# Cached keys through a bfloat16 copy and transposing DMAs, an earlier K^T for the first head, and eight PSUM banks for the first gate

## The chip, the cores and the metric

The program runs on the 8 cores of one Trainium2 chip, each core by itself: there is no traffic between them. The time is the device time of the slowest core, in microseconds. Each of the four prompt streams is shared by a pair of cores. The even core of a pair (role 0) owns the first 19 blocks of 128 frames and the two sample streams of the pair. The odd core (role 1) owns the last 13 blocks and recomputes the keys and values of the 19 before. Only the even cores hold cached keys.

## The reference, cut to what matters

```python
h = rmsnorm(x);  z = h @ w_in                 # columns: q | k | v | f | g_A | u | v_B | g_B
# A) forgetting attention, 8 heads x 128
logf = log_sigmoid(z_f + b_f);  cum = cumsum(logf)
s = (q @ k.T) * 128**-0.5 + cum[t] - cum[s];  p = softmax(causal(s));  att = p @ v
#    sample rows (16 per stream): k, v and logf are the 2048 cached rows, then the new ones
# B) gMLP: gelu(u) * (tril(W_s) @ LN(gelu(v_B)) + b), per 128-chunk and channel group
y = x + concat(att * silu(g_a), B * silu(g_B)) @ w_out;  y = rmsnorm(y)
```

The outputs are y, k, v, logf of prompt and sample rows and the sample's normalised v_B. Inputs are float32; matmul operands are bfloat16.

## The kernel before, in words

`emit` writes the instructions of one role by hand, engine by engine. Each engine executes its own list in order, and semaphores tie the lists. A DMA issued by SP or by POOL waits, in that queue, for its semaphores; what is listed behind it waits too. Only POOL's DMAs cast; the transposing DMAs (`tload`, line 131 of the helper) are all on SP. PSUM has 8 banks; `next_bank` hands them out in turn from the range in `banks`.

The stages of an even core, with `no` = 19 blocks and `ns` = 2 sample streams:

1. **K and V** (up to about 350 us): norm, transposes, K and V of each block. K goes to a bfloat16 scratch `K_s` in DRAM, row by row, V to `V_s`.
2. **v_B** (`b_front`, `b_back`, to about 510 us): v_B of each block, kept in SBUF as `vn`.
3. **The chunks** (`for ci in range(1, 17)`): 16 column chunks of w_in, alternately u and g_B of a channel group, each 80 matmuls (L581). The weights come by POOL's casting DMAs into a ring of 4 slots, so that a load is issued four chunks ahead. After each u chunk `mixing(gi - 1)` does a channel group's 128-chunk mixing: 19 matmuls (L860) and one for the sample rows (L868), in 6 calls of `next_bank` (banks 0 to 5), and on DVE three operations for each of them (L876, L877, L879); SP stores the result (`oT_s`).
4. **Crossing to attention**: `mixing(7)`; the attention's buffers are placed (`take_kv`, a write to a place waits for the earlier users of it); `e_loads(0)` on SP fetches the first head's K^T (transposing DMAs from `K_s`, 2432 and 32 rows) and V; POOL fetches the cached rows of both streams, `kc_load` and `vc_load`, 2048 rows of 128 float32 each, cast on the way; then the first head's gate, `ga_groups`: 20 blocks in 5 groups of 64 matmuls (L945), each group in one bank, evicted by ACT (tanh, L957) and DVE (L959). Here `banks` is set to 6 and 7. SP then fetches the query-side sums of the first two tiles (`cq_load`, from `CQ_s`), which DVE's diagonal step (L1156) reads.
5. **Attention**: per head a list of units, `hu`: 50 off-diagonal and 19 diagonal ones in six query tiles (4, 3, 3, 3, 3, 3 blocks), and 8 for the samples: `ktc0`, `ktc1` (8 PE transposes each of the cached K, L1118, and a DVE copy, L1164, to `KTc`), `smpS` (16 score matmuls, L1124) and `smpO` (16 matmuls, L1133, and a short DVE chain). Scores rotate through banks 0 to 2; the products with V (L1213) follow 5 units later (`LPV`) into bank 3 for off-diagonal and bank 4 for diagonal units; 7 units later (`LACC`) `fin_acc` reads them (L1081, L1084, L1086). Among the units of head h, `fill_upto` spreads 402 pieces of filler: the q projection (80 matmuls, L581) and the gate (320, L945) of head h + 1, with two ring loads. The last head has no filler. Loads for head h + 1 are issued at fixed unit positions: K^T and V at 9, the cached rows at 4, 18, 40 and 54.
6. **Output**: at the first unit of head 7 POOL issues the 16 loads of w_out (`wo_loads`), into the place of the dead H; near the head's end SP fetches the mixed rows (`g_load`, `oT_s` as it is and `o_s` by a transposing DMA). Then 1280 matmuls (L1336) and the final norm.

The lines that fix what the change touches:

```python
banks.update(lo=6, hi=8)                                   # before the first gate
for pos, kd, i in ((0, "ktc0", 0), (1, "ktc1", 0), (8, "smpS", 0), (14, "smpO", 0),
                   (36, "ktc0", 1), (37, "ktc1", 1), (44, "smpS", 1), (50, "smpO", 1)):
    hu.insert(pos, dict(kind=kd, h=h, st=i))
if u["pos"] == 9 and h + 1 < 8: e_loads(h + 1)
for pos, ld, st_ in ((4, kc_load, 0), (18, vc_load, 0), (40, kc_load, 1), (54, vc_load, 1)): ...
```

Of the kernel before, what the change touches and what calls it, by code (L numbers as in the profile page):

```python
# [137 lines left out]
class Chip:  # L138


    def __init__(self):
# [65 lines left out]
def emit(C, role):  # L207
# [674 lines left out]

    EB = W0 + 2 * QS + 2 * QS + 4096 + 512
# [219 lines left out]
    def e_S(i):  # L1103
# [5 lines left out]
        if k in ("off", "diag"):  # L1109
# [4 lines left out]
                  reads=[R_KTh[p], R_Qh[p]], writes=[PSR[bk]])  # L1114
        elif k in ("ktc0", "ktc1"):
            half = int(k[3])
            for j in range(8):
                PE.op(lambda j=j: nc.tensor.transpose(PSB[bk][:, :].bitcast(BF16)[:, j * 128:(j + 1) * 128], kc[u["st"]][:, half * 8 + j, :], S["ident_b"][:, :]),  # L1118
                      reads=[R_kc[u["st"]], R["ident_b"]], writes=[PSR[bk]] if j == 0 else [], pwrites=[] if j == 0 else [PSR[bk]], sig=(j == 7))
        elif k == "smpS":  # L1120
            c0 = no * 128 + u["st"] * NS
# [17 lines left out]
    def e_soft(i):  # L1139
# [5 lines left out]
        if k in ("off", "diag"):  # L1145
# [324 lines left out]
```

How the kernel before makes its waits and increments, by code:

```python
    def _wait(self, ev):  # L68
        sem, val = ev
        if sem is self.sem and self.is_pe:
            return
        if self.seen.get(id(sem), 0) >= val:
            return
        self.eng.wait_ge(sem, val)
        self.seen[id(sem)] = val
# [32 lines left out]
    def op(self, fn, reads=(), writes=(), pwrites=(), sig=True):  # L108
        self._deps(reads, writes, pwrites)
        ins = fn()
        if sig:
            ins.then_inc(self.sem, 1)
            self.cnt += 1
            ev = (self.sem, self.cnt)
        else:
            ev = (self.sem, self.cnt + 1)
        self._update(ev, reads, writes, pwrites)
        return ev
# [1 line left out]
    def dma(self, out, in_, dsem, reads=(), writes=(), pwrites=()):  # L120
        self._deps(reads, writes, pwrites)
        self.eng.dma_start(out=out, in_=in_).then_inc(dsem.sem, 16)
        dsem.cnt += 16
        ev = (dsem.sem, dsem.cnt)
        self._update(ev, reads, writes, pwrites)
        return ev
# [1 line left out]
    def dmat(self, out, in_, dsem, reads=(), writes=(), pwrites=()):  # L128
        self._deps(reads, writes, pwrites)
        self.eng.dma_start_transpose(out=out, in_=in_).then_inc(dsem.sem, 16)
        dsem.cnt += 16
        ev = (dsem.sem, dsem.cnt)
        self._update(ev, reads, writes, pwrites)
        return ev
```

## Time and profile before

| | |
|---|---|
| median of 3 runs | 1607.96 us (1606.09 to 1791.97) |
| the profiled execution | 1603.71 us, span 1600.1 us (core 2) |
| even cores | 1596.8, 1600.1, 1599.0, 1598.4 us |
| odd cores | 1564.7, 1561.2, 1562.9, 1561.4 us |
| busy on core 2 | PE 95 %, ACT 40 %, DVE 38 %, POOL 15 % |
| costliest lines | L581 419.1 us, L1336 278.7, L945 216.7, L1151 (ACT) 210.1, L1213 176.8, L1113 173.7 |

The profile is of core 2, the slowest. A busy time counts a matmul from its start to its modelled end, and matmuls overlap, so the time from one start to the next is what PE pays. In a timeline, "x128" merges 128 like instructions and the bracket gives the idle time before the first of them and what ended it. Line numbers are those of the kernel before.

### The profile page before, as it was taken

How to read it: one execution, taken by the hardware profiler on the slowest of the kernel's cores; microseconds unless marked ns; L12 is line 12 of the kernel's file. 1: busy time of each engine (PE TensorE's matmuls, PEld its weight loads, DVE VectorE, ACT ScalarE, POOL GpSimd, SP SyncE). 2: the span in 40 equal slices, each digit the busy share in tenths (PEclk: the TensorE clock that was granted, in tenths of full speed). 3: DMA queues.
4: the chain of work that ended last, by engine and by line, in shares of the span. 5: the costliest groups of instructions: out<-in, count | busy, mean ns of one | idle time of the engine just before them, and what ended most of it. 6: DMA issues, size and time to landing. Idle time of an engine off the chain costs nothing.

```text
span 1600.1 us, 31906 instructions; the slowest of 8 cores (1561.2 to 1600.1 us)
## 1 busy us (share of the span) xinstructions
PE 1515.2 (95%) x11367; PEld 887.4 (55%) x11367; DVE 600.4 (38%) x1276; ACT 642.5 (40%) x1331; POOL 247.1 (15%) x361
## 2 busy tenths in 40 slices
PE   3899999999999999999989999999999879999998
PEld 1455556554444444444568678677687644444443
DVE  1323222104444023322434445444444534544444
ACT  1222322214565222222227566566565652333332
POOL 5111111140333100000021212221111300000000
PEclk9999999999999999999999999999999899999999
DMA  9965445296000334333398877958846798756752
GB/s 188 232 196 179 178 168 181 109 191 80 1 1 1 40 43 56 44 58 49 50 161 109 117 90 111 116 68 122 102 68 97 122 225 210 226 151 207 188 160 90
DMA packets 266853, 191.38 MB, mean 120 GB/s; under 512 B 224762, under 2 KB 236194, under 8 KB 261634
## 3 DMA queue, kind: packets, MB, share of 16 engines
q1 hardware_dynamic: 125378, 134.69, 30.1%
q0 software_dynamic: 141312, 54.57, 29.7%
q8 instruction: 96, 1.57, 0.4%
q14 instruction: 67, 0.55, 0.1%
HBM read 172.85 MB, written 60.84 MB: 146 GB/s over the span
## 4 chain that ended last, share of the span: by engine, by line
PE 88%; DMA 6%; DVE 1%; ACT 1%; issue 1%; POOL 1%; another core or an unknown queue 0%; SPq 0%; POOLq 0%; DVEq 0%; ACTq 0%
PE psb L581 25%; PE psb L1336 17%; PE psb L785 9%; PE psb L440 8%; PE psb L430 8%; PE psb L945 7%; PE psb L1213 5%; PE psb L1113 5%; DMA arena<-w_in 2%; DMA o_s<-arena 1%; POOL arena L122 1%; PE psb L1133 1%; PE psb L415 1%; DMA arena<-oT_s 1%; DMA arena<-x_own 1%
## 5 line engine op out<-in xcount | busy, mean ns | idle before, releaser
L581 PE MATMUL psb<-arena 128*128 128x496 bf16 (+1 forms) x1920 | 419.1, 372 | 3.2 <-ACT psb L795 2.8
L581 PEld LDWEIGHTS psb<-arena 128*128 128x128 bf16 x1920 | 183.7, 98 | 194.8 <-issue 6.4
L1336 PE MATMUL psb<-arena 128*128 128x512 bf16 (+1 forms) x1280 | 278.7, 381 | 3.7 <-DMA arena<-oT_s 3.7
L1151 ACT ACTIVATE arena<-psb,offb 128x384 bf16<-128x384 f32 x400 | 210.1, 582 | 51.6 <-PE psb L1113 41.2
L945 PE MATMUL psb<-arena 128*128 128x128 bf16 (+1 forms) x2560 | 216.7, 220 | 4.3 <-DVE arena L959 4.3
L1336 PEld LDWEIGHTS psb<-arena 128*128 128x128 bf16 (+1 forms) x1280 | 125.6, 98 | 156.4 <-issue 7.1
L1213 PE MATMUL psb<-arena 128*128 128x129 bf16 x1520 | 176.8, 221 | 14.2 <-DVE arena L1081 7.9
L1113 PE MATMUL psb<-arena 128*128 128x384 bf16 (+3 forms) x552 | 173.7, 315 | 8.1 <-ACT arena L1151 3.7
L945 PEld LDWEIGHTS psb<-arena 128*128 128x128 bf16 (+1 forms) x2560 | 164.0, 98 | 11.9 <-issue 4.4
L430 PE MATMUL psb<-arena 128*128 128x512 bf16 (+1 forms) x640 | 147.4, 389 | 21.8 <-DMA arena<-w_in 15.4
L440 PE MATMUL psb<-arena 128*128 128x344 bf16 (+1 forms) x960 | 146.1, 311 | 7.0 <-DMA arena<-w_in 3.0
L1213 PEld LDWEIGHTS psb<-arena 128*128 128x128 bf16 x1520 | 124.1, 98 | 49.1 <-issue 17.0
L785 PE MATMUL psb<-arena 128*128 128x512 bf16 (+1 forms) x640 | 138.6, 379 | 0.0
L598 ACT ACTIVATE arena<-psb 128x496 bf16<-128x496 f32 (+1 forms) x120 | 69.3, 577 | 167.4 <-PE psb L581 166.4
L440 PEld LDWEIGHTS psb<-arena 128*128 128x128 bf16 (+1 forms) x960 | 93.4, 98 | 54.9 <-issue 10.0
L1361 ACT ACTIVATE arena<-arena 128x512 bf16<-128x512 f32 (+1 forms) x80 | 50.3, 629 | 175.2 <-DVE arena L1359 175.2
L430 PEld LDWEIGHTS psb<-arena 128*128 128x128 bf16 (+1 forms) x640 | 63.3, 99 | 99.7 <-issue 30.6
L1156 DVE SCALAR_TENSOR_TENSOR arena<-psb,cumn,arena 128x128 f32<-128x128 f32 (+3 forms) x152 | 74.2, 496 | 100.9 <-PE psb L1213 79.9
L122 POOL DMA_DIRECT2D arena<-w_in x80 | 64.4, 850 | 274.6 <-PE psb L860 124.6
L785 PEld LDWEIGHTS psb<-arena 128*128 128x128 bf16 (+1 forms) x640 | 62.4, 98 | 76.1 <-issue 1.2
L1159 ACT ACTIVATE arena<-arena 128x128 bf16<-128x128 f32 (+3 forms) x152 | 63.6, 426 | 95.8 <-DVE arena L1156 90.2
L876 DVE TENSOR_TENSOR arena<-psb,arena 128x512 f32<-128x512 f32 (+2 forms) x48 | 27.8, 579 | 185.3 <-PE psb L860 185.3
(151 smaller groups left out, 1202.7 us busy)
## 6 DMA issues: line engine op xcount, KB each, us to landing
arena<-x_own SPq DMA_DIRECT2D x38, 1024.0 KB, 6.9
y_own<-arena SPq DMA_DIRECT2D x38, 512.0 KB, 4.7
arena<-w_in POOLq DMA_DIRECT2D x32, 512.0 KB, 6.5
k_own<-arena SPq DMA_DIRECT2D x19, 512.0 KB, 3.7
v_own<-arena SPq DMA_DIRECT2D x19, 512.0 KB, 2.8
arena<-w_in POOLq DMA_DIRECT2D x32, 256.0 KB, 15.7
arena<-ck POOLq DMA_DIRECT2D x16, 512.0 KB, 8.0
arena<-cv POOLq DMA_DIRECT2D x16, 512.0 KB, 8.8
```

The lines of the kernel that those rows point to most:

```text
L122: self.eng.dma_start(out=out, in_=in_).then_inc(dsem.sem, 16)
L430: PE.op(lambda k=k, c=c: mm(PSB[2 + c][0:rows, :], hT[:, k, :], WK[:, k, c * 512:(c + 1) * 512], start=(k == 0), stop=(k == KC - 1)), read ...
L440: PE.op(lambda k=k, c=c: mm(PSB[4 + c][0:rows, 0:VC], hT[:, k, :], WV[:, k, c * VC:(c + 1) * VC], start=(k == 0), stop=(k == KC - 1)), rea ...
L581: PE.op(lambda: mm(PSB[bk][:, 0:n], wt[:, k, :], H[:, k, c0:c0 + n], start=(k == 0), stop=(k == KC - 1)), reads=rh + [r_wt], writes=[PSR[b ...
L598: ACT.op(lambda: act(out=dst[:, c0:c0 + n], in_=PSB[bk][:, 0:n], func=func), reads=[PSR[bk]], writes=[r_dst] if ti == 0 else [], pwrites=[ ...
L785: PE.op(lambda k=k, c=c: mm(PSB[pb + c][0:rows, :], H[:, k, c0:c0 + rows], WVB[k][:, c * 512:(c + 1) * 512], start=(k == 0), stop=(k == KC ...
L945: PE.op(lambda: mm(PSB[bk][0:rows, jj * 128:(jj + 1) * 128], H[:, k, j * 128:j * 128 + rows], wt[:, k, :], start=(k == 0), stop=(k == KC - ...
L1113: PE.op(lambda: mm(PSB[bk][:, o:o + n], KTh[p][:, gk * 128:(gk + 1) * 128], Qh[p][:, q0 + o:q0 + o + n], start=True, stop=True), reads=[R_ ...
L1151: ACT.op(lambda: act(out=Pb[pi][:, 0:n], in_=PSB[bk][:, 0:n], func=AF.Exp, scale=SCALE, bias=S["offb"][:, t["oo"] + u["g"], h:h + 1]), rea ...
L1156: DVE.op(lambda: v.scalar_tensor_tensor(out=dt[di][:, 0:n], in0=PSB[bk][:, o:o + n], scalar=S["cumn"][:, t["b0"] + u["i"], h:h + 1], in1=c ...
L1213: PE.op(lambda: mm(PSB[bk][:, c0:c0 + 129], Pb[pi][:, a * 128:(a + 1) * 128], Vh[p][:, u["g"], 0:129], start=first, stop=True, skip_group_ ...
L1336: PE.op(lambda: mm(PSB[bk][0:rows, :], oT[op_][:, k, j * 128:j * 128 + rows], wo[k][:, cg * 512:(cg + 1) * 512], start=(ki == 0), stop=(ki ...
```

## The change

- In the chunks 1 to 8, POOL copies a quarter of one stream's cached K (512 rows of 1024, float32) to a new scratch `kc_s` in DRAM, cast to bfloat16: eight copies, on even cores alone.
- `kc_load` becomes a transposing DMA on SP from `kc_s` straight to `KTc`, which now has one buffer for each stream; the units `ktc0` and `ktc1` go (four units in each of the 8 heads), with their buffers `kc`. The `smpS` units move to the head's start (0 and 1; in the first head 12 and 13), the `smpO` units to 20 and 26; the loads move to 15, 16 (K) and 28, 40 (V).
- `e_loads` is split. The first head's K^T, `KTh0`, has a place of its own and is fetched after chunk 12.
- The first gate takes all eight banks, from bank 6 on (6, 7, 0, 1, 2); the narrowing to banks 6 and 7 follows it.
- The attention's buffers are placed in another order, and on odd cores the last w_out rows and the output buffers move.

```diff
+        self.kc_s = dscr("kc_s", [NSMAX * PAST, 1024], BF16)
...
-    bsb, R_bsb = b.take("bsb", [128], F32)
-    assert b.off <= W0 + 32768
+    EA = b.off
+    KTh0, R_KTh0 = b.take("KTh0", [nk * 128 + NR], BF16)
+    EK = b.off
+    assert EK <= W0 + 32768
...
+    def e_kloads(h):
+        p = h % 2
+        tload(KTh[p][:, 0:nk * 128].unsqueeze(1), C.K_s[0:nk * 128, h * 128:(h + 1) * 128], R_KTh[p], extra=[R_Ks])
+        if ns:
+            tload(KTh[p][:, nk * 128:nk * 128 + NR].unsqueeze(1), C.K_s[NKEY:NKEY + NR, h * 128:(h + 1) * 128], R_KTh[p], extra=[R_Ks], part=True)
...
         ring_load()
+        if ci == 12:
+            e_kloads(0)
+        if ns and ci <= ns * 4:
+            r0 = (ci - 1) * (PAST // 4)
+            POOL.dma(C.kc_s[r0:r0 + PAST // 4, :], C.ck[r0:r0 + PAST // 4, :], dsem_of(R_kcs), pwrites=[R_kcs])
...
     mixing(7)
-    banks.update(lo=6, hi=8)
-    take_kv(0)
+    banks.update(lo=0, hi=8, n=6)
...
+    assert b.off <= EA
+    b.off = EK
+    take_v(0)
...
+        KTc, R_KTc = b.many("KTc", ns, [PAST], BF16)
...
-    e_loads(0)
+    e_vloads(0)
 
     def kc_load(h, i):
-        load(POOL, kc[i][:, :, :], C.ck[i * PAST:(i + 1) * PAST, h * 128:(h + 1) * 128].rearrange("(b t) c -> t b c", t=128), R_kc[i])
+        tload(KTc[i][:, :].unsqueeze(1), C.kc_s[i * PAST:(i + 1) * PAST, h * 128:(h + 1) * 128], R_KTc[i], extra=[R_kcs])
...
     for f in ga_groups(ring[17 % NSLOT], R_ring[17 % NSLOT], GAh[0], R_GAh[0]):
         f()
+    banks.update(lo=6, hi=8)
     ring_load()
...
-            for pos, kd, i in ((0, "ktc0", 0), (1, "ktc1", 0), (8, "smpS", 0), (14, "smpO", 0),
-                               (36, "ktc0", 1), (37, "ktc1", 1), (44, "smpS", 1), (50, "smpO", 1)):
+            for pos, kd, i in ((12 if h == 0 else 0, "smpS", 0), (13 if h == 0 else 1, "smpS", 1), (20, "smpO", 0), (26, "smpO", 1)):
...
-        elif k in ("ktc0", "ktc1"):
-            half = int(k[3])
-            DVE.op(lambda: v.tensor_copy(out=KTc[:, half * 1024:(half + 1) * 1024], in_=PSB[bk][:, :].bitcast(BF16)),
-                   reads=[PSR[bk]], writes=[R_KTc] if half == 0 else [], pwrites=[] if half == 0 else [R_KTc])
...
             if u["pos"] == 9 and h + 1 < 8:
-                e_loads(h + 1)
+                e_kloads(h + 1)
+                e_vloads(h + 1)
             if ns and h + 1 < 8:
-                for pos, ld, st_ in ((4, kc_load, 0), (18, vc_load, 0), (40, kc_load, 1), (54, vc_load, 1)):
+                for pos, ld, st_ in ((15, kc_load, 0), (16, kc_load, 1), (28, vc_load, 0), (40, vc_load, 1)):
```

## Rows read from the trace of the kernel before

**Rows 1.** Spans and granted clock of the cores, one odd and the slowest even.

```profile
core 1: 1564.7 us, clock 0.991
...
core 2: 1600.1 us, clock 0.988
```

**Rows 2.** Chain of waits, core 2, 817 to 1260: shares by line, two head starts.

```profile
by line: PE psb L581 26.3%; PE psb L945 26.2%; PE psb L1213 17.1%; PE psb L1113 16.0%; PE psb L1133 3.3%; PE psb L1118 3.0%; issue 1.9%; ACT arena L957 1.3%; PE psb L1124 1.2%; ACT arena L1151 0.9%; DVE arena L1081 0.9%; DVE arena L1156 0.4
...
1133.63 1.26 PE psb L581 x6
...
1197.07 1.26 PE psb L581 x6
```

**Rows 3.** Timeline, core 2, the last head and the first output matmuls.

```profile
1260.77 8.51 POOL L122 DMA_DIRECT2D arena<-w_out  x16 [0.24 <-issue]
...
1270.01 0.59 PE L1213 MATMUL psb<-arena 128*128 128x129 bf16 x4 [4.18 <-POOL arena L1160]
...
1314.27 2.29 PE L1336 MATMUL psb<-arena 128*128 128x512 bf16 x5 [3.66 <-DMA arena<-oT_s]
```

**Rows 4.** DMA queues, core 2, 1260 to 1316 (queue: packets, MB, share).

```profile
DMA packets 9203, 11.64 MB, mean 208 GB/s; under 512 B 5611, under 2 KB 7147, under 8 KB 9195
...
q0 software_dynamic: 2304, 8.39, 76.5%
```

**Rows 5.** Timeline, core 2, last mixing and first gate (start us, us, engine line op).

```profile
791.40 7.32 PE L945 MATMUL psb<-arena 128*128 128x128 bf16 x128
...
801.39 0.18 DVE L876 TENSOR_TENSOR arena<-psb,arena 128x32 f32<-128x32 f32 x1
...
802.15 1.28 DVE L959 SCALAR_TENSOR_TENSOR arena<-arena,psb 128x512 bf16<-128x512 f32 x2
...
802.98 12.61 PE L945 MATMUL psb<-arena 128*128 128x128 bf16 x192 [4.26 <-DVE arena L959]
...
816.95 0.61 PE L1118 MATMUL psb<-ident_b,arena 128*128 128x128 bf16 x8 [1.36 <-DMA arena<-ck]
```

**Rows 6.** Windows, core 2 (stretch, length, busy by engine, PEclk, DMA share, GB/s).

```profile
668.00:703.00 35.00, 35.00 (x183) 17.01 (x182) 10.09 (x18) 8.37 (x12) 2.28 (x2) 1.00 0.37 49
...
802.00:817.00 15.00, 12.66 (x193) 12.44 (x194) 3.36 (x6) 1.68 (x3) 6.71 (x11) 0.89 1.11 161
```

**Rows 7.** Chain of waits, core 2, 1197 to 1320: one transpose unit.

```profile
1198.33 0.45 PE psb L1118 x8
```

**Rows 8.** Line 131, core 2: issue time on SP of each transposing load.

```profile
L131 SPq DMA_TRANSPOSE arena<-K_s x16: 1205/1824/8440, 803.1 to 1212.7; - x16
```

**Rows 9.** DMA issues, core 2 (count, KB each, median us to landing).

```profile
arena<-ck POOLq DMA_DIRECT2D x16, 512.0 KB, 8.0
...
arena<-K_s SPq DMA_TRANSPOSE x16, 4.7
```

**Rows 10.** Timeline of SP's DMA queue, core 2: issues at 803 to 814 and 893.

```profile
803.06 5.66 SPq L131 DMA_TRANSPOSE arena<-K_s  x2
...
814.38 11.92 SPq L122 DMA_DIRECT2D arena<-CQ_s  x4
...
893.23 3.69 SPq L131 DMA_TRANSPOSE arena<-K_s  x2
```

**Rows 11.** Waits of PE, core 2, 817 to 1320 (total us, times, longest).

```profile
PE psb L1213 <- DVE arena L1081: 7.9, 7, 1.3
```

**Rows 12.** Timeline, core 2, one such wait in the head that began at 943.

```profile
974.02 0.69 DVE L959 SCALAR_TENSOR_TENSOR arena<-arena,psb 128x512 bf16<-128x512 f32 x1 [2.46 <-ACT arena L957]
...
974.63 0.55 DVE L1081 TENSOR_TENSOR arena<-psb,Ecol 128x387 f32<-128x387 f32 x1
...
975.33 0.33 PE L1213 MATMUL psb<-arena 128*128 128x129 bf16 x3 [1.08 <-DVE arena L1081]
```

**Rows 13.** Timeline of DVE, core 2: end of a sample's epilogue in the last head.

```profile
1294.82 0.28 DVE L1188 TENSOR_TENSOR arena<-psb,arena 32x129 f32<-32x129 f32 x1
...
1295.96 0.34 DVE L1193 SCALAR_TENSOR_TENSOR arena<-arena 32x128 bf16<-32x128 f32 x1 [0.17 <-DVE arena L1192]
```

More of the change, by code:

```diff
@@ L299, in emit @@
     R_tz = [Res("tz%d" % i) for i in range(33)]
-    R_Ks, R_Vs, R_CQs = Res("K_s"), Res("V_s"), Res("CQ_s")
+    R_kcs, R_Ks, R_Vs, R_CQs = Res("kc_s"), Res("K_s"), Res("V_s"), Res("CQ_s")
     R_oTg = [Res("oT_g%d" % k) for k in range(8)]
@@ L881, in mixing @@
         store(SP, C.oT_s[gi, :, 0:TO], ob[p][:, :], R_ob[p], R_oTg[gi])
-    EB = W0 + 2 * QS + 2 * QS + 4096 + 512
+    KTh, R_KTh = [KTh0], [R_KTh0]
+    def e_kloads(h):
[3 more added lines that the diff above has]
+            tload(KTh[p][:, nk * 128:nk * 128 + NR].unsqueeze(1), C.K_s[NKEY:NKEY + NR, h * 128:(h + 1) * 128], R_KTh[p], extra=[R_Ks], part=True)
     for ci in range(1, 17):
@@ L899, in emit, with take_v @@
     b = Bump(W0)
-    KTh, Vh, R_KTh, R_Vh = [], [], [], []
+    Vh, R_Vh = [], []
     def ones_col(ap, r, n):
         pool(lambda: g.memset(ap[:, 0:n, 128:129], 2.0), writes=[r])
-    def take_kv(i):
-        a, r = b.take("KTh%d" % i, [nk * 128 + NR], BF16)
-        KTh.append(a); R_KTh.append(r)
+    def take_v(i):
         a, r = b.take("Vh%d" % i, [nk + 1, VW], BF16)
@@ L910, in take_kv, with e_vloads @@
         ones_col(a, r, nk + 1)
-    def e_loads(h):
+    def e_vloads(h):
         p = h % 2
-        tload(KTh[p][:, 0:nk * 128].unsqueeze(1), C.K_s[0:nk * 128, h * 128:(h + 1) * 128], R_KTh[p], extra=[R_Ks])
-        if ns:
-            tload(KTh[p][:, nk * 128:nk * 128 + NR].unsqueeze(1), C.K_s[NKEY:NKEY + NR, h * 128:(h + 1) * 128], R_KTh[p], extra=[R_Ks], part=True)
         first = True
@@ L966, in emit @@
     mixing(7)
-    banks.update(lo=6, hi=8)
-    take_kv(0)
+    banks.update(lo=0, hi=8, n=6)
     th, R_th = b.many("th", 2, [512], F32)
     cqt, R_cqt = b.many("cqt", 3, [512], F32)
-    NPB = 12
-    Pb, R_Pb = b.many("Pb", NPB, [512], BF16)
     dt, R_dt = b.many("dt", 2, [512], F32)
-    tt, R_tt = b.many("tt", 2, [4, VW], F32)
-    rcs, R_rcs = b.many("rcs", 2, [8], F32)
     os_, R_os = b.many("os", 3, [4, 128], BF16)
     if ns:
-        kc, R_kc = b.many("kc", ns, [16, 128], BF16)
-        vc, R_vc = b.many("vc", ns, [16, VW], BF16)
-        KTc, R_KTc = b.take("KTc", [PAST], BF16)
+        rcs, R_rcs = b.many("rcs", 2, [8], F32)
+        tt, R_tt = b.many("tt", 2, [4, VW], F32)
         st, R_sst = b.take("sst", [256 + NR], F32)
-        Ps, R_Ps = b.many("Ps", ns, [16, NR], BF16)
         Pn, R_Pn = b.take("Pn", [NR], BF16)
@@ L985, in emit @@
         sob, R_sob = b.take("sob", [128], BF16)
+    assert b.off <= EA
+    b.off = EK
+    take_v(0)
+    if not ns:
+        rcs, R_rcs = b.many("rcs", 2, [8], F32)
+        tt, R_tt = b.many("tt", 2, [4, VW], F32)
+    NPB = 12
+    Pb, R_Pb = b.many("Pb", NPB, [512], BF16)
+    if ns:
+        KTc, R_KTc = b.many("KTc", ns, [PAST], BF16)
+        vc, R_vc = b.many("vc", ns, [16, VW], BF16)
+        Ps, R_Ps = b.many("Ps", ns, [16, NR], BF16)
         for i in range(ns):
@@ L988, in emit @@
             pool(lambda: g.memset(Ps[i][:, :, :], 0.0), writes=[R_Ps[i]])
-    take_kv(1)
+    a, r = b.take("KTh1", [nk * 128 + NR], BF16)
+    KTh.append(a); R_KTh.append(r)
+    take_v(1)
     EEND = b.off
@@ L1114, in e_S @@
                   reads=[R_KTh[p], R_Qh[p]], writes=[PSR[bk]])
-        elif k in ("ktc0", "ktc1"):
-            half = int(k[3])
-            for j in range(8):
-                PE.op(lambda j=j: nc.tensor.transpose(PSB[bk][:, :].bitcast(BF16)[:, j * 128:(j + 1) * 128], kc[u["st"]][:, half * 8 + j, :], S["ident_b"][:, :]),
-                      reads=[R_kc[u["st"]], R["ident_b"]], writes=[PSR[bk]] if j == 0 else [], pwrites=[] if j == 0 else [PSR[bk]], sig=(j == 7))
         elif k == "smpS":
@@ L1123, in e_S @@
             for j in range(16):
-                PE.op(lambda j=j: mm(PSB[bk][:, j * NS:(j + 1) * NS], KTc[:, j * 128:(j + 1) * 128], Qh[p][:, c0:c0 + NS], start=True, stop=True),
-                      reads=[R_KTc, R_Qh[p]], writes=[PSR[bk]] if j == 0 else [], pwrites=[] if j == 0 else [PSR[bk]], sig=(j == 15 and not lastst))
+                PE.op(lambda j=j: mm(PSB[bk][:, j * NS:(j + 1) * NS], KTc[u["st"]][:, j * 128:(j + 1) * 128], Qh[p][:, c0:c0 + NS], start=True, stop=True),
+                      reads=[R_KTc[u["st"]], R_Qh[p]], writes=[PSR[bk]] if j == 0 else [], pwrites=[] if j == 0 else [PSR[bk]], sig=(j == 15 and not lastst))
             if lastst:
@@ L1161, in e_soft @@
                                              fill=0.0, base=0, channel_multiplier=-1), reads=[R_Pb[pi]], writes=[R_Pb[pi]])
-        elif k in ("ktc0", "ktc1"):
-            half = int(k[3])
-            DVE.op(lambda: v.tensor_copy(out=KTc[:, half * 1024:(half + 1) * 1024], in_=PSB[bk][:, :].bitcast(BF16)),
-                   reads=[PSR[bk]], writes=[R_KTc] if half == 0 else [], pwrites=[] if half == 0 else [R_KTc])
         elif k == "smpS":
@@ L1229, in wo_loads @@
         for i, k in enumerate(KORD):
-            wo[k], R_wo[k], _ = place("wo%d" % k, i * 4096, [D], BF16)
+            nh = HB // 4096
+            wo[k], R_wo[k], _ = place("wo%d" % k, i * 4096 if i < nh else EA + (i - nh) * 4096, [D], BF16)
             R_wo[k].dsem = mkdsem("wo%d" % (i // 2))
@@ L1324, in emit @@
     assert not pending
-    b = Bump(65536 if wide else 65536 + 2 * 8192)
+    wend = 65536 if HB >= 65536 else EA + (KC - HB // 4096) * 4096
+    b = Bump(wend if wide else wend + 2 * 8192)
     xr[1], R_xr[1] = b.take("xr1", [D], F32)
-    yb, R_yb = b.many("yb", 2, [D], F32)
+    yb, R_yb = (b if HB >= 65536 else Bump(W0)).many("yb", 2, [D], F32)
     junk, R_junk = b.take("junkF", [512], BF16)
     oT[1], R_oT[1] = b.take("oT1", [16, 512], BF16, parts=2)
+    assert HB >= 65536 or (wide and W0 + 16384 <= EA and b.off <= EEND)
     R_ssF = [Res("ssF%d" % i) for i in range(2)]
```

## The prediction

> **What bounds the kernel now.** I read the cores first. The even cores end last, core 2 at 1600.1 us, and the odd ones at about 1565 [rows 1]. Only even cores have cached keys, so the change acts where the end is set, and nothing it does there can bring the time below what the odd cores need: 1564.7 plus the 3.6 us that lie between span (1600.1) and time (1603.71) of the profiled execution, 1568.
>
> Then the chain of waits of core 2, stretch by stretch. From 817 to 1260, seven heads, nearly all of the chain is PE's own work: the reader is to see that the q projection, the gate, scores and products lead, that the transposes (L1118) have 3.0 % of it and that waits on other engines are about a percent each [rows 2]. Two heads start 63.4 us apart [rows 2]. What PE no longer does there is won, one for one, as long as nothing else becomes late.
>
> The last head is another matter. It has no filler, and its end is set by w_out: POOL issues the 16 loads from 1260.77 on, 8.39 MB go through in 56 us at three quarters of the DMA engines' time, and the output matmuls begin at 1314.27, after a wait on a DMA [rows 3, 4]. PE's work in between is not on the path.
>
> The crossing from the chunks to attention has two waits of PE: 4.26 us within the first gate and 1.36 us on the cached rows before the first transposes [rows 5].
>
> **The change, part by part.**
>
> *The transposes.* A unit of eight takes 0.45 us of the chain [rows 7]; that agrees with 3.0 % of 443 us, 13.3 us, for the 30 units of that stretch [rows 2]. Heads 0 to 6 lose 28 units: 28 x 0.45 = 12.6 us. The Trainium skill (TensorE: Matmul & The Clock Gate, Part 4: PE-mode transpose) gives about 275 ns for a transpose in a kernel's context; by it the sum would be 28 x 8 x 0.275 = 61.6 us. The row decides: the eight run pipelined, 0.45 us together. In head 7 the four units are worth nothing: its first PE wait, 4.18 us, ends when POOL has issued w_out [rows 3], and its last is the DMA's. The DVE copies go too; DVE is no bound.
>
> *The gate on eight banks.* Before, the third group of 64 waits until the first two are evicted, and their evictions stand in DVE's list behind all of the last mixing [rows 5]. After, the groups take banks 6, 7, 0, 1, 2. But bank 0 is not free early. Counting `next_bank` on an even core (5 for the first projection, 16 x 5, 7 x 6 = 127), the six calls of the last mixing take banks 1, 2, 3, 4, 5, 0: its last piece, the sample rows, is in bank 0, and DVE reads it at 801.39 for 0.18 us [rows 5]. So the third group starts at about 801.7 instead of 802.98: **1.3 us**, not 4.3. The gap stays near 3 us. The granted clock in 802 to 817 averages 0.89 [rows 6]: after the gap part of the group runs at 1.2 GHz, which costs 0.11 x 15 = 1.7 us. I take that to stay, and its worth as the bound above.
>
> *The cached keys.* The wait of 1.36 us falls away: the first unit becomes a diagonal one, whose K^T landed long before and whose queries are in SBUF. POOL's 16 loads, 8.0 us to landing each, go; 16 transposing loads on SP come. The nearest row is K_s itself, 2432 rows of the same layout: SP is held 1.2 to 8.4 us, median 1.8, landing after 4.7 [rows 8, 9]; for 2048 rows I take 3 us each, near the undisturbed pair of 3.69 [rows 10]. Queued behind them on SP are stores of `o_s` (three buffers) and `cq_load`s issued two tiles ahead, more than 10 us of work; K^T and V for the next head are needed some 50 us later. Even 2 x 8.4 us is covered, in heads 1 to 6. In the crossing SP's order is: mixing's store (802.2), V, two key loads, then the first tile's `cq_load`. Before, K^T held SP there for 5.66 us, the 5.7 from its end to 814.38 went to V, and then came `cq_load` [rows 10]; after, V 3 to 6 and keys 4 to 9 put it at 810 to 817, and I allow it 4 us to land, near the 4.7 of a key load [rows 9]. DVE's first diagonal step needs it; PE goes on for three units of 1.25 us, to 818, before a score bank is missing. I take no loss, and 0 to 4 us as the bound. If V is late, PE notices at the sixth unit, 820.5.
>
> *The copies.* No row shows a DMA from DRAM to DRAM. The nearest with the same cast are POOL's w_out loads: 8.39 MB at 76.5 % of 56 us is 196 GB/s [rows 4], so 1.05 MB would take 5.4 us in a chunk of 17 us, whose DMA share is 0.37 [rows 6]. POOL pays about 0.5 us an issue (8.51 for 16 [rows 3]) and is idle there. The ring's weights are queued up to three chunks, 50 us, ahead. Cost nothing; the upper bound is the third rival. K^T for head 0 goes out after chunk 12 behind a mixing's store, with 65 us to spare.
>
> *The order of the units.* Once per head PE waits for DVE's L1081, seven times, 7.9 us in all [rows 11]: the gate's L959, waiting for ACT, stands ahead of it [rows 12]. The filler's group ends move with the head's length: 402 pieces over 77 units end the first gate group at unit 27, one unit before that `fin_acc` (28); over 73 units both fall on unit 26, and `fin_acc` is issued first. But `smpO` of the second stream now stands at 26 too, and its DVE chain, about 1.5 us from the first to the last step [rows 13], precedes `fin_acc`. PE reaches the product that needs the bank 1.7 us after `smpO`, DVE frees it after some 2.4: a wait of about 0.7 instead of 1.1. Taken: 7 x 0.4 = 2.5 us; bounds 7.9 gained and 3 lost. Two `smpS` at the head's start share one buffer, so DVE waits there for ACT once; PE's units are 1.25 us long there and cover it.
>
> *Places.* The output's buffers now overlie others; what they wait for (the last stores of head 7) ends before DVE's first addition is due, 14 us after 1314 (64 matmuls of 278.7 / 1280 us). Nothing.
>
> **Sum:** 12.6 + 1.3 + 1.4 + 2.5 = 17.8 us. 1603.7 - 17.8 = 1585.9 against the profiled execution, which lies 4.3 us below the median shown; 1607.96 - 17.8 would be 1590.2. I predict **1588**. By the bounds the gain is 12.6 + 4.4 + 7.9 = 24.9 at best, 12.6 - 4 - 3 + 1.3 = 7 at worst: 1577 to 1601.
>
> **Rivals.** 1. *The work removed turns into new waits.* `cq_load` late in the crossing, DVE's chain before `fin_acc`, key loads delaying a head's first units: with 2 us lost per head and 4 in the crossing, 18 us are gone and the time is 1600 to 1608. For it: the first head's pair of K^T loads did hold SP up to 8.4 us [rows 8]. Against: DMA gets less work, not more, since loads that land after 8.0 us are replaced by ones of 4.7 [rows 9]. Chance 0.15.
>
> 2. *Faster by more than 2 %* (the bound I use throughout, 32 us of 1608, about what a measurement here can tell from no change). PE would have to pay 0.97 us for a transpose unit ((32.2 - 5.2) / 28), or every remaining wait would have to go: 5.4 us of L1081, 1.7 of clock and the chain's 1.9 % of issue, 8.4 us, make 33 and 1571. The odd cores end it at 1568. The skill's 275 ns above would be 2.2 us a unit and lead to that floor. The 0.45 us of a unit [rows 7] speaks against. Chance 0.05.
>
> 3. *Slower: the copies are not ready.* SP waits for all eight before the first key load, at about 807, and the first tile's `cq_load` stands behind it, so PE stops at 818 until they land. They start at about 530 (15 chunks of 17.3 us before 790): the point is 34 us a copy. At 45 us they end at 890 and the time is near 1660. If one of the 16 engines did each copy, 196 / 16 = 12 GB/s, 85 us each, the stop would be some 400 us. The Trainium skill (DMA: Bandwidth & Descriptors, Why a DMA increments its semaphore by 16 and not by 1) has the engines chosen by the outermost dimension, the largest divisor up to 16; 512 rows would then use all. No row here shows such a copy. Chance 0.04.
>
> 4. *No effect:* another even core or wait holds the end. The even cores lie within 4 us and do the same work; 0.02, at 1606.
>
> **Chances.** The forecast 0.74 (1577 to 1598), rivals 0.15, 0.05, 0.04, 0.02. The range 1576 to 1602 takes the forecast's bounds and most of rival 1. Faster 0.05 (rival 2), slower 0.05 (rival 3 and a hundredth of rival 1), within 2 % 0.90.
>
> **What would show it.** No L1118; the third gate group after a gap near 2.9 us, on DVE's L876; the first scores at about 814; heads of 61 us; L1081 waits fewer or shorter; 1314 less the gain for the first output matmul, and some 53 us from w_out's first issue to it, as before. Wrong would be: PE waiting for CQ_s or V at 815 to 825, heads of 63 us, or a chunk stage that stretches beside the copies.

## The result, and the profile after

The changed kernel takes 1587.1 us (median of 4) against 1607.0 for the kernel before beside it, a ratio of 0.988 with a 95 % interval of [0.987, 0.990]. Timed again on another chip it was 1588.4 against 1609.8, 0.987 [0.985, 0.989]. That is 1.2 to 1.3 % faster, within the 2 % called no change, and 1 us from the 1588 forecast. Medians of different sittings differ by some us, so kernels are compared below by these ratios and by their traces. The medians take in every execution; the ratios leave out those in which the cores of a die ran at a lower clock and took longer.

The profiled execution took 1584.46 us; the even cores still end last [rows 1].

```profile
core 0: 1580.9 us, clock 0.988
core 1: 1553.0 us, clock 0.993
core 2: 1580.0 us, clock 0.991
```

Where the 20.1 us of core 2 went (span 1600.1 to 1580.0), stage by stage, each from the starts of the same instructions in the two timelines (the end of the last mixing is the start of its last matmul):

| stage, core 2 | before | after | difference |
|---|---|---|---|
| to the end of the last mixing | 791.3 | 791.9 | +0.6 |
| last mixing to the first q projection of head 0 | 26.1 | 21.6 | -4.5 |
| head 0 | 63.0 | 62.1 | -1.0 |
| heads 1 to 6, to w_out's first issue | 380.3 | 364.8 | -15.5 |
| w_out's first issue to the first output matmul | 53.5 | 52.9 | -0.6 |
| output and final norm | 285.8 | 286.7 | +0.9 |

A head in the steady state, from the chain of waits of core 2 (start, us, what): 60.64 us apart where [rows 2] has 63.44 (63.2 between most other heads).

```profile
1057.89 1.26 PE psb L582 x6
...
1118.53 1.25 PE psb L582 x6
```

The wait on `fin_acc` is shown first in PE's waits between 870 and 1240 (total, times, longest), then at one such place in the timeline. It was 1.08 us a time [rows 12], and is 0.39: the sample unit's last step on DVE (L1201) now stands ahead of `fin_acc` (L1098), and the gate's product (L969) behind it.

```profile
PE psb L1221 <- DVE arena L1098: 2.3, 6, 0.4
```

```profile
967.55 0.34 DVE L1201 SCALAR_TENSOR_TENSOR arena<-arena 32x128 bf16<-32x128 f32 x1 [0.17 <-DVE arena L1200]
967.82 0.54 DVE L1098 TENSOR_TENSOR arena<-psb,Ecol 128x387 f32<-128x387 f32 x1
968.29 0.67 DVE L969 SCALAR_TENSOR_TENSOR arena<-arena,psb 128x512 bf16<-128x512 f32 x1
968.51 0.33 PE L1221 MATMUL psb<-arena 128*128 128x129 bf16 x3 [0.39 <-DVE arena L1098]
```

The crossing, timeline of core 2, is to be held against [rows 5] and [rows 10]. The third gate group starts after 3.00 us instead of 4.26, when DVE has read the sample rows out of bank 0. The 192 matmuls from there to the gate's end take 10.98 us instead of 12.61. Then SP's order shows: the two cached-key loads hold it for 5.65 us, `cq_load` goes out at 813.70, DVE gets it at 818.05, and PE, after three score units with their filler, stands still for 1.50 us.

```profile
791.99 7.32 PE L955 MATMUL psb<-arena 128*128 128x128 bf16 x128
...
801.99 0.18 DVE L879 TENSOR_TENSOR arena<-psb,arena 128x32 f32<-128x32 f32 x1
802.32 10.98 PE L955 MATMUL psb<-arena 128*128 128x128 bf16 x192 [3.00 <-DVE arena L879]
807.78 5.65 SPq L131 DMA_TRANSPOSE arena<-kc_s  x2
813.70 8.36 SPq L122 DMA_DIRECT2D arena<-CQ_s  x4
818.05 1.28 DVE L1168 SCALAR_TENSOR_TENSOR arena<-psb,cumn,arena 128x512 f32<-128x512 f32 x2 [2.59 <-DMA arena<-CQ_s]
818.95 0.22 PE L1130 MATMUL psb<-arena 128*128 128x128 bf16 x1 [1.50 <-DVE arena L1168]
```

Core 0 of the same execution is the slowest. It reached the crossing 2.8 us earlier than core 2; `cq_load` went out at 810.95 and still took until 817.91, so that PE waited 4.17 us.

```profile
805.54 5.14 SPq L131 DMA_TRANSPOSE arena<-kc_s  x2
810.95 10.98 SPq L122 DMA_DIRECT2D arena<-CQ_s  x4
817.91 1.27 DVE L1168 SCALAR_TENSOR_TENSOR arena<-psb,cumn,arena 128x512 f32<-128x512 f32 x2 [5.26 <-DMA arena<-CQ_s]
818.81 0.27 PE L1130 MATMUL psb<-arena 128*128 128x128 bf16 x1 [4.17 <-DVE arena L1168]
```

The windows behind it (length, busy by engine, PEclk, DMA share, GB/s), core 0 and then core 2: on core 0 the granted clock is 0.86 after the wait, so part of these 10 us ran at 1.2 GHz; on core 2, after 1.50 us, it stayed at 1.00.

```profile
819.00:829.00 10.00, 10.00 (x54) 4.93 (x53) 1.57 (x4) 6.29 (x12) 1.18 (x4) 0.86 0.83 110
```

```profile
819.00:829.00 10.00, 10.00 (x61) 5.13 (x62) 2.19 (x5) 7.17 (x14) 1.46 (x5) 1.00 0.95 132
```

Last, the end of attention on core 2, which is as it was [rows 3]: 52.9 us from w_out's first issue to the first output matmul, with a POOL wait and a DMA wait in it.

```profile
1240.34 8.53 POOL L122 DMA_DIRECT2D arena<-w_out  x16 [0.24 <-issue]
1249.43 0.59 PE L1221 MATMUL psb<-arena 128*128 128x129 bf16 x4 [3.48 <-POOL arena L1172]
...
1293.23 7.14 PE L1348 MATMUL psb<-arena 128*128 128x512 bf16 x19 [3.92 <-DMA arena<-oT_s]
```

### The profile page after: what moved, and what is told of

Read it like the earlier page. It is cut to its first block, busy times and chain, and to the rows that moved or that the text cites. A ratio compares the mean times of both kernels' runs of the same rounds, so it can differ in the third digit from the quotient of the medians.

```text
span 1580.9 us, 31319 instructions; the slowest of 8 cores (1548.5 to 1580.9 us)
## 1 busy us (share of the span) xinstructions
PE 1497.7 (95%) x11047; PEld 872.4 (55%) x11111; DVE 578.2 (37%) x1244; ACT 650.7 (41%) x1331; POOL 232.6 (15%) x353
## 4 chain that ended last, share of the span: by engine, by line
PE 88%; DMA 5%; DVE 2%; issue 2%; ACT 1%; POOL 1%; SPq 1%; DVEq 0%; POOLq 0%; ACTq 0%; another core or an unknown queue 0%
PE psb L582 25%; PE psb L1348 18%; PE psb L786 9%; PE psb L441 8%; PE psb L955 8%; PE psb L431 8%; PE psb L1221 5%; PE psb L1130 5%; DMA arena<-w_in 2%; PE psb L1145 1%; DMA v_own<-arena 1%; DMA arena<-oT_s 1%; PE psb L416 1%; DMA arena<-x_own 1%; POOL arena L122 1%
## 5 line engine op out<-in xcount | busy, mean ns | idle before, releaser
L1163 ACT ACTIVATE arena<-psb,offb 128x384 bf16<-128x384 f32 x400 | 215.8, 584 | 35.8 <-PE psb L1130 25.6
L955 PE MATMUL psb<-arena 128*128 128x128 bf16 (+1 forms) x2560 | 211.8, 219 | 3.0 <-DVE arena L879 3.0
L1130 PE MATMUL psb<-arena 128*128 128x384 bf16 (+2 forms) x544 | 171.2, 315 | 11.5 <-DVE arena L1168 7.7
L431 PE MATMUL psb<-arena 128*128 128x512 bf16 (+1 forms) x622 | 146.0, 394 | 22.8 <-DMA arena<-w_in 14.8
L955 PEld LDWEIGHTS psb<-arena 128*128 128x128 bf16 (+1 forms) x2560 | 160.9, 98 | 10.8 <-issue 3.2
L1172 POOL TENSOR_SCALAR_AFFINE_SELECT arena<-arena 128x128 bf16<-128x128 bf16 x152 | 44.5, 296 | 374.1 <-ACT arena L1171 372.8
## 6 DMA issues: line engine op xcount, KB each, us to landing
arena<-w_in POOLq DMA_DIRECT2D x32, 256.0 KB, 15.7
```

The source lines that it names most:

```text
L431: PE.op(lambda k=k, c=c: mm(PSB[2 + c][0:rows, :], hT[:, k, :], WK[:, k, c * 512:(c + 1) * 512], start=(k == 0), stop=(k == KC - 1)), read ...
L955: PE.op(lambda: mm(PSB[bk][0:rows, jj * 128:(jj + 1) * 128], H[:, k, j * 128:j * 128 + rows], wt[:, k, :], start=(k == 0), stop=(k == KC - ...
L1130: PE.op(lambda: mm(PSB[bk][:, o:o + n], KTh[p][:, gk * 128:(gk + 1) * 128], Qh[p][:, q0 + o:q0 + o + n], start=True, stop=True), reads=[R_ ...
L1163: ACT.op(lambda: act(out=Pb[pi][:, 0:n], in_=PSB[bk][:, 0:n], func=AF.Exp, scale=SCALE, bias=S["offb"][:, t["oo"] + u["g"], h:h + 1]), rea ...
```

## The experiments

All are edits of the changed kernel. The theory to test is this: the transposes and the shorter `fin_acc` wait were won in full, while the crossing's gains were partly lost again to the wait for `cq_load`. The rivals stand in each expectation.

### The queries' sums ahead of the cached keys

```diff
     for i in range(ns):
-        kc_load(0, i)
         vc_load(0, i)
...
     cq_load(tlist[0])
     cq_load(tlist[1])
+    for i in range(ns):
+        kc_load(0, i)
```

> The changed kernel with one reordering on SP's queue: the first two tiles' cq loads are issued ahead of head 0's two cached-key loads instead of behind them. Theory A (what the faster gate wins in the crossing is given back in part as a wait for cq, because the key loads hold SP for 5.1 to 5.7 us ahead of it): cq lands near 811 us, PE's wait for the first diagonal step (1.50 us on core 2, 4.17 on core 0) goes, head 0 is shorter by as much and nothing else moves, since the cached keys are needed only at head 0's units 12 and 13, 15 us later: 1.5 to 4 us off the changed kernel's time, most on core 0. Theory B (the wait is hidden anyway: PE would have waited for the score pipeline's start there, whatever releases it): the wait is named differently but stays, within 0.5 us of the changed kernel.

Measured: 1583.2 us, 0.986 [0.984, 0.988]. Timeline of core 0: `cq_load` leaves SP at 806.98, DVE begins at 813.48 with no wait, and PE's fourth score unit follows without one. The key loads now take 11.37 us of SP, and nobody waits for them.

```profile
806.98 0.81 SPq L122 DMA_DIRECT2D arena<-CQ_s  x2
807.94 11.37 SPq L131 DMA_TRANSPOSE arena<-kc_s  x2
813.48 1.28 DVE L1169 SCALAR_TENSOR_TENSOR arena<-psb,cumn,arena 128x512 f32<-128x512 f32 x2
...
815.32 0.22 PE L1131 MATMUL psb<-arena 128*128 128x128 bf16 x1
```

None of the four even cores waits there, and head 0 takes 60.3 to 60.7 us instead of 62.1 to 66.2. This is theory A. By the ratios it is worth 1.3 to 3 us, but the intervals overlap: the verdict rests on the trace.

### The first gate on two banks again, with the sums late and with them early

```diff
-    banks.update(lo=0, hi=8, n=6)
+    banks.update(lo=6, hi=8)
```

> The changed kernel with the first gate on banks 6 and 7 alone, as before the change. Theory A (cq sets when the scores go on, the gate does not): the gap before the third group returns to about 4.3 us, the granted clock falls behind it again, the gate ends some 2.9 us later, the wait for cq shrinks by as much, and the time moves by 0 to +1.4 us on core 2, 0 on core 0. Theory B (gains add up): +2.9 us.

> Both edits: cq loads ahead of the cached-key loads, and the first gate on banks 6 and 7. Theory A: with cq out of the way the gate is worth its full 2.9 us (1.3 of gap and 1.6 of clock), so this is about 2.9 us slower than the kernel with the cq loads first alone. Theory B (the clock after the gap is chance and not the gap's length): only the 1.3 us of gap.

### The first gate without bank 0, the sums early

```diff
-    banks.update(lo=0, hi=8, n=6)
+    banks.update(lo=1, hi=8, n=5)
```

> cq loads first, and the first gate on banks 6, 7, 1, 2, 3 instead of 6, 7, 0, 1, 2. Theory A (the 3.0 us gap before the third group is the wait for bank 0, where the sample rows of the last mixing stand until DVE reads them): the gap goes altogether, the gate ends some 3 us earlier than in the kernel with the cq loads first alone, and the time is lower by up to 3 us, less if the V load or the cq load becomes what the first tile waits for. Theory B (the third group waits for anything else, as DVE's whole list or the gate's weights): the gap stays at 3 us and the time too.

The three are read together with the one before, on the four even cores of the profiled executions: the gate's length (end of the last mixing to the start of the gate's last matmul), the wait for `cq_load`, and the stretch from the last mixing to the start of head 1, which holds both. The last row is the repeated run of the changed kernel, shown below.

| kernel | gate, us | wait for cq, us | mixing to head 1, us |
|---|---|---|---|
| before | 24.0 to 24.1 | none | 89.1 to 89.7 |
| changed | 21.2, 21.2, 22.8, 22.8 | 4.2, 1.5, 1.6, 1.8 | 87.8, 83.6, 85.3, 85.6 |
| two banks | 23.9 to 24.1 | 2.7, 0, 0, 0.7 | 89.1, 85.2, 84.8, 86.4 |
| sums early | 21.2, 22.8, 21.2, 22.8 | none | 82.3, 83.5, 81.9, 83.5 |
| sums early, two banks | 24.0 to 24.1 | none | 84.7, 84.8, 84.7, 85.2 |
| sums early, no bank 0 | 18.0 on all four | none | 79.1, 80.4, 80.9, 79.0 |
| changed, again | 22.8, 22.8, 21.2, 21.2 | 0.5, 1.9, 5.3, 3.9 | 84.3, 85.7, 90.2, 87.6 |

With the sums early the eight banks are worth 2.0 us (mean of the last column 84.8 less 82.8), with the sums late about 0.1 (86.4 against 86.3 over the two runs of the changed kernel): what PE saves in the gate it waits out behind it, as theory A has it for the late sums. Of the two theories for the early sums each holds on two cores: the gate is 2.9 us shorter on two (theory A) and 1.2 on the two others (theory B), because the clock's part is won on some cores only. In times: two banks 1586.2 us, 0.987 [0.985, 0.989]; with the sums early 1584.9, 0.987 [0.986, 0.989].

Without bank 0 the five groups run as one, 320 matmuls in 18.14 us on core 2 at full clock. Next to it the same place with bank 0 and with two banks, the sums early in all three, each a timeline of core 2:

```profile
791.14 18.14 PE L955 MATMUL psb<-arena 128*128 128x128 bf16 x320
```

```profile
800.86 12.61 PE L955 MATMUL psb<-arena 128*128 128x128 bf16 x192 [3.01 <-DVE arena L879]
```

```profile
803.96 12.61 PE L955 MATMUL psb<-arena 128*128 128x128 bf16 x192 [4.27 <-DVE arena L969]
```

So the 3.0 us were the wait for the sample rows in bank 0, and nothing else: theory A. The time, 1581.4 us, 0.988 [0.981, 0.995], is too wide to tell, because one execution took 1597.9 us; the stretch from the mixing to head 1 is 2.9 us shorter in the mean.

### The transposes put back in heads 0 to 6

```diff
             lastst = u["st"] == ns - 1
+            if u["h"] < 7:
+                for j in range(16):
+                    PE.op(lambda j=j: nc.tensor.transpose(PSB[bk][:, :].bitcast(BF16)[:, (j % 8) * 128:(j % 8 + 1) * 128], KTc[u["st"]][:, j * 128:(j + 1) * 128], S["ident_b"][:, :]), ...)
```

> The changed kernel with extra work: in heads 0 to 6 each of the two cached-key score units first does 16 PE transposes of the cached K into its own score bank, which the scores then overwrite; there is no DVE copy and no extra wait, so this is the transposes' price for PE alone. Theory A (they are paid by the row, 0.45 us for eight, and all of it lies on PE's path): 28 x 0.45 = 12.6 us slower than the changed kernel, heads 62.4 us apart instead of 60.6. Theory B (what the changed kernel won per head came from waits of other engines that went with the units, and the pipelined transposes are cheaper or hidden): under 8 us. Theory C (a transpose costs PE what the Trainium skill's page TensorE: Matmul & The Clock Gate, Part 4: PE-mode transpose, gives for one in a kernel's context, about 275 ns): 61.6 us.

Measured: 1601.4 us, 0.9945 [0.9925, 0.9964], clear of the changed kernel's interval. The chain of core 2 has heads 62.43 us apart against 60.64, 1.79 us for four units of eight, 0.45 each, as in [rows 7]; in heads 1 to 6 it is so on all even cores.

```profile
1012.69 1.26 PE psb L582 x6
...
1075.12 1.25 PE psb L582 x6
```

Seven heads make 12.5 us. This is theory A; B's "under 8" and C's 61.6 are out. By the ratios the time is only 10 to 12 us above the changed kernel's, and their intervals also cover 12.5.

### The transposes put back in head 7 alone

```diff
+            if u["h"] == 7:
```

> The same extra transposes in head 7 alone, 32 of them, 1.8 us of PE at 0.45 us for eight. Theory A (head 7's end is set by w_out's loads and what queues with them, not by PE): the first output matmul stands as far behind the first w_out issue as without them, 52 to 53.5 us, and the time is within 0.5 us of the changed kernel's. Theory B (PE's own chain sets head 7's end too): +1.8 us.

Measured: 1589.0 us, 0.9895 [0.9862, 0.9928]. Timeline of core 2:

```profile
1241.75 8.52 POOL L122 DMA_DIRECT2D arena<-w_out  x16 [0.24 <-issue]
1250.83 0.59 PE L1225 MATMUL psb<-arena 128*128 128x129 bf16 x4 [3.63 <-POOL arena L1176]
...
1295.36 4.81 PE L1352 MATMUL psb<-arena 128*128 128x512 bf16 x13 [4.76 <-DMA arena<-oT_s]
```

PE gets past POOL's wait 9.08 us after w_out's first issue, with 32 transposes more, and 9.09 without them: up to there they cost nothing. They fill time in which PE waited for DVE anyway: its short waits ahead of POOL's add up to 3.0 us without them and 1.6 with them. The first output matmul comes 53.6 to 54.5 us after the issue, mean 54.2; in the two runs of the changed kernel 52.9 to 54.3, mean 53.6. That is beyond the 53.5 that theory A allowed, and a third of B's 1.8. The place is the DMA's as forecast; whether half a microsecond belongs to the transposes is not settled.

### The second sample product later

```diff
-(20, "smpO", 0), (26, "smpO", 1)):
+(20, "smpO", 0), (30, "smpO", 1)):
```

> The changed kernel with the second stream's product unit at unit 30 of a head instead of 26. Theory A (PE's steady wait of 0.39 us a head ends when DVE frees the accumulator, and DVE is late because that unit's vector chain stands ahead of the accumulator's in its list): the waits for fin_acc in heads 1 to 6 go to zero, heads are 60.25 instead of 60.64 us apart, 2.3 to 2.7 us in all. Theory B (DVE is late for the accumulator whatever stands ahead, by the gate's eviction for instance): the wait stays or moves, within 0.5 us of the changed kernel.

Measured: 1588.6 us, 0.9865 [0.9843, 0.9887]. The waits on `fin_acc` are gone from PE's list between 870 and 1240, and many heads are 60.36 us apart. But heads 1 to 6 together gain 0.8 us (364.0 against 364.8, mean of the even cores), not 2.3: some heads stay at 60.64, and the score matmuls (L1130) get a wait of 0.49 in head 6. In head 7 the later unit costs 0.6 before the first output. A is right on the cause of the wait and wrong on the gain.

### The mixed rows fetched before w_out

```diff
             if u["hfirst"] and u["h"] == 7:
+                f_early()        # places oT0, g_load(0, (1,))
                 wo_loads()
...
-        g_load(0)
+        g_load(0, (0,))          # the o_s half alone
```

> The changed kernel with the mixed rows of the first output group (1 MB from the oT scratch) fetched at the first unit of head 7, ahead of w_out's loads on the DMA engines, instead of near the head's end. Theory A (the first output matmul waits 3.9 us for these rows alone, since they were issued late behind w_out's packets): the wait goes, and the next late thing is the transposed attention rows or the last normalisation; the first output matmul comes 2 to 3.9 us earlier. Theory B (what sets the head's end is the total traffic of 8.4 MB of w_out and the rest on the DMA engines, in whatever order): moving 1 MB ahead delays the other loads by as much, and the first output matmul stays within 1 us.

Measured: 1586.6 us, 0.9858 [0.9837, 0.9879]. On core 2 the wait of 3.9 us is gone and the output begins 50.3 us after w_out's first issue:

```profile
1242.03 8.52 POOL L122 DMA_DIRECT2D arena<-w_out  x16 [0.24 <-issue]
...
1292.31 7.89 PE L1352 MATMUL psb<-arena 128*128 128x512 bf16 x28 [0.34 <-issue]
```

On the four even cores it is 49.4 to 51.2, mean 50.2 against 53.6: theory A. The median does not show the 3.5 us. In the profiled execution core 0 waited 5.7 us for `cq_load`, fell behind and ended last, at 1582.0; the three others ended at 1573.3 to 1577.6.

### Each copy made twice

```diff
             POOL.dma(C.kc_s[r0:r0 + PAST // 4, :], C.ck[r0:r0 + PAST // 4, :], dsem_of(R_kcs), pwrites=[R_kcs])
+            POOL.dma(C.kc_t[r0:r0 + PAST // 4, :], C.ck[r0:r0 + PAST // 4, :], dsem_of(R_kct), pwrites=[R_kct])
```

> The changed kernel with each of the eight copies of the cached K made twice, the second time to another scratch that nobody reads. Theory A (the copies cost nothing, because the chunks' weights are queued three chunks ahead and the DMA engines have room): the pitch of two chunks beside the copies stays at 34.6 us, and the time is within 1 us of the changed kernel's. Theory B (the copies are near the edge of what the chunk stage hides): each copy takes 10 us to land and the DMA engines are busy 4 to 7 tenths in those slices already; at 8 tenths or more the weights come late, the pitch grows by up to 5 us a chunk, 40 us in all.

Measured: 1588.6 us, 0.988 [0.986, 0.990]. Core 2 from 540 to 700, the changed kernel and then this one: the DMA share goes from 0.62 to 0.91, and PE does the same 824 matmuls in the same busy time.

```profile
540.00:700.00 160.00, 159.60 (x824) 77.29 (x823) 40.38 (x72) 38.26 (x55) 14.26 (x16) 1.00 0.62 97
```

```profile
540.00:700.00 160.00, 159.59 (x824) 77.32 (x823) 40.43 (x72) 38.49 (x56) 17.68 (x23) 1.00 0.91 150
```

The pitch of two chunks is 34.58 us before the change, with the copies and with twice the copies. This is theory A; even a DMA share of nine tenths did not delay a chunk.

### The edits together

The sums early, the gate without bank 0 and the mixed rows early; then the same with the second sample product at unit 30 in heads 0 to 6.

> Three edits together: cq loads ahead of head 0's cached-key loads, the first gate on banks 6, 7, 1, 2, 3, the mixed rows of the first output group fetched ahead of w_out. Theory A (each removes a wait of its own, at three places of PE's path): against the changed kernel 1.5 to 4 us for the cq wait on the slowest core, 3.2 to 4.8 for the gap and the clock behind it, 3 for the rows, some 8 to 10 us, 1577 to 1579 by the changed kernel's 1587. Theory B (they pass the wait on to the next late transfer): no more than the 4 us that the first two gave together.

> The same three edits, and the second stream's product unit at unit 30 in heads 0 to 6 (26 in head 7, which has no filler to cover what the move delays there). Theory A: 0.28 us a head for most of seven heads, 1.5 to 2 us less than the three edits alone. Theory B (a wait of 0.3 to 0.6 us moves to other units): no difference.

Measured: 1577.8 us, 0.9804 [0.9787, 0.9822], beside 0.9870 [0.9850, 0.9891] for the changed kernel in the same sitting: 10.6 us faster than the change and 2.0 % faster than before. With the sample product moved it is 1579.3, 0.9814 [0.9794, 0.9834]: no difference that the times show, as theory B has it. The traces have heads 1 to 6 at 364.1 us instead of 365.0 (mean of the even cores), half of theory A's gain. With the three edits alone, core 2 begins the output 48.4 us after w_out's issue; the even cores need 48.4 to 51.7, and from the last mixing to head 1 78.8 to 80.6.

```profile
1235.35 8.53 POOL L122 DMA_DIRECT2D arena<-w_out  x16 [0.24 <-issue]
...
1283.79 8.54 PE L1353 MATMUL psb<-arena 128*128 128x512 bf16 x31 [0.40 <-issue]
```

Three waits of a few us, at three places, do add up (theory A: 8 to 10 us, 1577 to 1579).

### The changed kernel once more

> The changed kernel itself once more, beside the others. Theory A (the wait for cq in the crossing is the key loads' time on SP, which swings from core to core and from execution to execution): the four even cores again show waits anywhere from 0 to 6 us before the fourth score unit, and the span differences of the even cores follow them. Theory B (the wait is fixed by the order of the instructions): 1.5 to 4.2 us on each core as before.

Measured: 1588.4 us, 0.987 [0.985, 0.989]. The waits are 0.5, 1.9, 5.3 and 3.9 us, on core 4 the longest, and core 4 ends last, at 1587.5, with the others at 1580 to 1582. Its timeline:

```profile
815.39 10.16 SPq L122 DMA_DIRECT2D arena<-CQ_s  x4
821.54 1.28 DVE L1168 SCALAR_TENSOR_TENSOR arena<-psb,cumn,arena 128x512 f32<-128x512 f32 x2 [6.37 <-DMA arena<-CQ_s]
...
822.44 0.27 PE L1130 MATMUL psb<-arena 128*128 128x128 bf16 x1 [5.28 <-DVE arena L1168]
```

The granted clock of the 10 us in which the wait ends is 0.66:

```profile
819.00:829.00 10.00, 6.56 (x24) 2.82 (x25) 2.04 (x4) 4.51 (x9) 1.17 (x4) 0.66 0.67 118
```

This is theory A. Over the eight profiled executions with the key loads first, 29 of 32 even cores wait there (27 of them 0.4 us or more), and the longest wait of each execution is 2.6 to 7.0 us; over the five with the sums first, one core of 20 waits, 0.6 us. The time is that of the slowest core, so it pays the longest of four draws, and a slower clock behind it: head 0 takes 60.3 us without a wait, 62.1 with 1.5, 66.2 with 4.2 and 68.6 with 5.3.

## Why the prediction was right

*The transposes: 12.6 us.* This is shown: putting them back costs 12.5. The row's 0.45 us was the price. By the 275 ns of the Trainium skill (TensorE: Matmul & The Clock Gate, Part 4: PE-mode transpose) it would have been an estimated 61.6 in the sum; the measured 12.5 decides against that for transposes that run one behind the other.

*Head 7 worth nothing.* This is shown up to POOL's release, to 0.01 us; behind it within 0.6 us. The two waits that bound this stretch are the ones named.

*The gate: 1.3 us.* The mechanism, bank 0 and its sample rows, is shown by leaving that bank out, and so is the gap of about 3 us. What failed is "I take that to stay" of the clock's 1.7 us: over all kernels whose gate waits 3.0 us for bank 0, 13 of 32 gates lost nothing to the clock, among them core 2's in the profile (10.98 us for 192 matmuls instead of 12.61). It was left as the bound, and should have been a term with a chance.

*The cached keys: 1.4 us.* The wait on `ck` is gone. The term that was mis-sized is `cq_load`: "I allow it 4 us to land", with "I take no loss, and 0 to 4 us as the bound". SP reached it when forecast (810 to 817; it was 813.70 on core 2 and 810.95 on core 0, behind key loads of 5.7 and 5.1 us). On core 2 PE ran out of score banks when forecast (818; it was 817.45), on core 0, which is ahead, at 814.64. But DVE began 4.35 us after the issue on core 2 and 6.96 on core 0, and PE's next score unit came 0.90 later still. Even with 4 us to land PE would have waited 1.2 us on either core, so "no loss" was too little; the rest is the landing. The row for it was not a key load's 4.7 [rows 9] but the same load's own, at the same place in the kernel before, where PE did not wait for it (DMA issues, core 2, 812 to 817: count, KB, us to landing):

```profile
arena<-CQ_s SPq DMA_DIRECT2D x1, 256.0 KB, 7.2
```

Why the load took longer on core 0 than on core 2 is not shown: on both, V and two key loads were issued ahead of it, and from 811 to 818 the DMA share was 1.08 on core 0 and 1.12 on core 2. The loss in head 0 of the profiled execution is 1.8 us on core 2 and 5.9 on core 0, clock included, and the second is outside the bound. "PE waiting for CQ_s or V at 815 to 825" was one of the prediction's own signs of being wrong, and it came. So on the slowest core the crossing's gains, 2.9 us at the gate and 1.4 at the cached keys, were gone: there the stretch from the last mixing to head 1 is 1.3 us shorter (89.1 to 87.8), less than the 1.8 us of head 0's transposes alone. Rival 1 named this place and 4 us for it; it happened there, and not in the heads that rival 1 had also named.

*The order of the units: 2.5 us.* It was right in kind (the sample unit's chain ahead of `fin_acc`, the gate's product behind it) and too small: 0.39 us a head are left instead of 0.7. Over heads 0 to 6 the waits of 7.9 us [rows 11] became 2.7 (0.32 in head 0, six times 0.39), a gain of 5.2.

*The copies: nothing.* This is shown with twice the copies. They took about 10 us to land (median 9.8 for the seven between 540 and 680 on core 2), not 5.4, and the point of 34 us at which rival 3 would have begun was never near.

*Key loads on SP.* They were forecast at 3 us each from [rows 8] and took 2.8 in the median; line 131, core 2 (issue time on SP in ns, least, median and most):

```profile
L131 SPq DMA_TRANSPOSE arena<-kc_s x16: 1872/2804/5971, 807.8 to 1202.0; - x16
```

No head waits for them after the crossing.

On core 2 the terms close: 17.8 forecast, 2.7 more from the order of the units, 1.6 more from the clock, 1.8 less for the late sums make 20.3, and its span fell by 20.1. The profiled execution fell by 19.3 (1603.71 to 1584.46), because core 0, with the longer wait, now ends last. So the sum of 17.8 held in part by luck: the gains were 4.3 us larger than forecast, and a wait that the sum put at nothing took 1.8 us of them back on core 2 and more on core 0.

## What to carry to other kernels

Loads moved onto a queue delay what stands behind them there, and at a crossing of stages the first small load that a whole chain needs goes ahead of large ones that are needed 15 us later. The time to allow a load is read from its own row at that place, not from another load's. In a program whose time is that of its slowest core, a wait that varies from core to core is paid at its longest, and it can pay again as clock. Several microsecond waits at separate places on one engine's path add up, even where none is seen by itself in the times.

## What the runs showed of the hardware

- **The clock behind a gap.** After the same wait of 3.0 us the gate's remaining 192 matmuls ran at 2.4 GHz throughout on 13 of 32 cores and in part at 1.2 GHz on 19 (10.98 or 12.61 us; in the profile of the change, from 802 to 814, the granted clock is 1.00 on core 2 and 0.88 on core 4); after 4.26 us they were slowed on 12 of 12 (12.41 to 12.61 us), and without a gap on none of 12.
- **Copies from DRAM to DRAM with a cast.** 1 MB out took 9.8 us to land, and alongside a second like it 10.4 and 15.7 (medians, core 2). A DMA share of 0.91 over 160 us left PE's 824 matmuls where they were.
- **Transposing loads.** 2048 rows of 128 held SP from 1.9 to 6.0 us each on core 2; over all kernels and even cores, the pair in the crossing held it 4.3 us at the least and 11.4 at the most.
- **Left open.** In some executions PE pauses 0.3 to 2.0 us within the gate of heads 0 to 3 (L955), with no wait that the profile shows, on cores and at units that change from run to run.
